# The first expert's row numbers taken from four one-hot tiles of their own, ahead of the routing table

## The chip, the cores and the metric

The kernel runs on one core of one Trainium2 chip. The metric is the device time of one execution in microseconds (us); less is better. The profile is one execution, taken by the hardware profiler, and its times count from the start of its span.

## The reference

Two requests of 256 tokens (512 tokens in four tiles of 128, D = 1024) pass two layers. Layer 0 mixes tokens by a bidirectional mLSTM, layer 1 by a gated short convolution; each mixer is followed by a layer norm, a mixture of experts and another layer norm.

```python
logits = (t @ router_w) + router_b                  # 16 experts in 4 groups of 4
probs = softmax(logits)
g_sel = argmax(sum of the two largest probs of each group)
top_v, top_i = top_k(probs inside group g_sel, 2)
gates = top_v / sum(top_v)
for e in range(16):
    gu = t @ w_gu[e]                                # 1024 -> 512
    h = silu(gu[:, :256]) * gu[:, 256:]
    out += combine[:, e] * (h @ w_down[e])          # 256 -> 1024
x = layer_norm(ALPHA * x + out)
```

## The kernel before

Every large product is made of three products of split operands (hi times hi, hi times lo, lo times hi). ScalarE writes the hi part of a weight unit (128x2048), VectorE the lo part, TensorE multiplies. The experts are computed sparsely: each token has two experts, every expert's tokens are gathered from DRAM into 128 places, multiplied, scaled by their gate and scattered back, and the scattered results are added later.

Between a mixer and its experts stands the router, once a layer. Its steps in order of the engines:

- TensorE ends `out_projection` with `logits(t)` (L710, fp32 products, two instructions each in the trace) and then `spin(6, 5)` (called at L742, recorded as L555). A spin is one product of the identity with 512 columns whose result nobody reads, again two instructions; it only fills TensorE's time.
- VectorE adds constants and takes the maximum (L1649 to L1653), ScalarE the exponential, and VectorE's `choose` finds each token's best group and its two experts with some 28 small instructions (L1671 to L1729). `step_done.wait(but=n)` lets an instruction start before the n latest ones have completed; `step_done.wait()` waits for all. The last one writes `chosen` and releases TensorE (`s_chosen`).
- TensorE's `router` computes every token's place within its experts (L762, L764), then `spin(1, 5)`. VectorE meanwhile writes `values` (token number and result row of every token and expert, L1658) and then reads the places (L1735, L1739).
- VectorE writes eight one-hot tiles of place numbers, one for each choice k and token tile t (L1743); TensorE multiplies each with `values` into a table of the row numbers of all 16 experts (`slot_table`, L779), then runs `spin(2, 5)`.
- VectorE takes the table to `rows_of` (L1748, `s_ix`). GpSimd waits for that and issues indirect DMAs that gather the tokens of expert 0 and expert 1 (L2026), and then weight loads of the next norm. SyncE's queue holds back two expert weight loads and all that follow until gather 0 has landed (L400).
- VectorE computes the gates (L1752 to L1757) and writes them by expert (L1658 again, `s_gv`); TensorE multiplies them with the same one-hot tiles (L779), runs `spin(4, 5)`, and then `tokens_T(0, 0)` transposes the gathered tokens of expert 0 (L795) and the experts begin (L823, later L495 and L852).

TensorE's instructions run in the order in which they are written, so `tokens_T(0, 0)` stands behind the gates' products and the four spins.

Of the kernel before, what the change touches and what calls it, by code (L numbers as in the profile page):

```python
# [5 lines left out]
ALU = mybir.AluOpType  # L6
# [35 lines left out]
def trunk(nc, gate_cols, router_cols, x_prompt, x_sample, router_w, router_b, mlstm_w_in, mlstm_b_gate, mlstm_norm_g, mlstm_w_out,  # L42
# [36 lines left out]
    with ctx:  # L79
        def sb(name, shape, dt=F32):  # L80
            return ctx.enter_context(nc.sbuf_tensor(name, shape, dt))

        def sem(name):
            return ctx.enter_context(nc.semaphore(name))
# [46 lines left out]
        chosen_pad = sb("chosen_pad", [P, 2 * NT + 1, E], F32R)  # L131
        chosen = chosen_pad[:, NT:2 * NT, :]
        place = sb("place", [P, 2, NT])
        facts = sb("facts", [P, 2, NT, 2], F32R)
        shares = sb("shares", [P, 2, NT, 2], F32R)
        r_max = sb("r_max", [P, 1])
# [46 lines left out]
                         for at in (2048, 2304))  # L183
        dn_hi, dn_lo = (of_flat(a)[:, 2048:4096] for a in (xt_hi, xt_lo))
        gate_w_hi, gate_w_lo = (of_flat(a)[:, 0:KC * 16].rearrange("p (k n) -> p k n", k=KC) for a in (h_hi, h_lo))
        zT = temp[:, 0:2048].rearrange("p (b c s) -> p b c s", b=2, c=KC)
        silu_g = temp[:, 1024:1536].rearrange("p (b f) -> p b f", b=2)
        h_tok = temp[:, 1536:2048].rearrange("p (b f) -> p b f", b=2)
# [96 lines left out]
        s_rank = sem("places_multiplied")  # L285
        s_routed = sem("routing_ready")
        s_oh = sem("one_hot_ready")
        s_ixm = sem("rows_multiplied")
        s_gv = sem("gates_by_expert_ready")
        s_gm = sem("slot_gates_multiplied")  # L290
# [200 lines left out]
        def _(pe):  # L491
# [60 lines left out]
            def spin(n, bank):  # L552

                for _ in range(n):
                    pe.matmul(ps[:, bank, :], ident[:, :], ident[:, :].unsqueeze(1).to_broadcast([P, 4, P]),  # L555
                              start=True, stop=True)
# [126 lines left out]
            def out_projection(layer, first_unit, ready, after=lambda kh, t: None):  # L683

                def part(half, kh, t):
                    tok = slice(t * P, (t + 1) * P)
                    for k in range(4):
                        w = slice(k * CG, (k + 1) * CG)
                        x = 4 * kh + k
                        ins = products(ps[:, 4 * half + t, :],  # L690
                                       [(xt_hi[:, x, tok], w_hi[:, kh, w]), (xt_hi[:, x, tok], w_lo[:, kh, w]),
                                        (xt_lo[:, x, tok], w_hi[:, kh, w])],
                                       kh == 0 and k == 0, kh == 1 and k == 3)
                    if t == 3:
                        ins.then_inc(s_hl, 1)
                    elif kh == 1:
                        ins.then_inc(s_bank, 1)

                def raw_T(t, half):
                    pe.wait_ge(s_sum, 2 * NT * layer + (t + 1 if half == 0 else NT + t + 1))  # L700
                    for c in range(4):
                        f0 = (4 * half + c) * P
                        ins = pe.transpose(ps[:, 4 * half + t, c * P:(c + 1) * P], z[:, t, f0:f0 + P], ident[:, :])  # L703
                    ins.then_inc(s_tr, 1)

                def logits(t):
                    for c in range(KC):
                        if c % 4 == 0:
                            pe.wait_ge(s_za, 2 * NT * layer + 2 * t + c // 4 + 1)
                        ins = pe.matmul(ps[:, t, 0:E], zT[:, t % 2, c, :], rout_c[:, layer, c, :],  # L710
                                        start=c == 0, stop=c == KC - 1)
                    ins.then_inc(s_lg, 1)

                for kh in range(2):
                    pe.wait_ge(s_lo, first_unit + kh + 1)
                    for t in range(NT):
                        ready(kh, t)
                        part(0, kh, t)
                        after(kh, t)
                pe.wait_ge(s_lo, first_unit + 3)  # L720
                part(1, 0, 0)
                part(1, 0, 1)
                pe.wait_ge(s_lo, first_unit + 4)
                part(1, 1, 0)
                part(1, 1, 1)
                part(1, 0, 2)
                raw_T(0, 0)
                raw_T(0, 1)
                part(1, 1, 2)
                raw_T(1, 0)  # L730
                raw_T(1, 1)
                logits(0)
                part(1, 0, 3)
                raw_T(2, 0)
                raw_T(2, 1)
                logits(1)
                raw_T(3, 0)
                part(1, 1, 3)
                logits(2)
                raw_T(3, 1)  # L740
                logits(3)
                spin(6, 5)  # L742

            def heads_ready(kh, t):
                pe.wait_ge(s_xtl, 8 + NT * kh + t + 1)
# [12 lines left out]
            def router(layer):  # L758

                pe.wait_ge(s_chosen, layer + 1)  # L760
                out = ps[:, 4, 0:(NT + 1) * E]
                pe.matmul(out, earlier[:, :], slots(NT), start=True, stop=False)  # L762
                for back in range(1, NT + 1):
                    ins = pe.matmul(out, all_ones[:, :], slots(NT - back), start=False, stop=back == NT)  # L764
                ins.then_inc(s_rank, 1)
                spin(1, 5)
                for n in range(2 * NT):
                    pe.wait_ge(s_oh, 2 * NT * layer + n + 1)
                    ins = slot_table(values, 0, n)
                ins.then_inc(s_ixm, 1)  # L770
                spin(2, 5)
                pe.wait_ge(s_gv, layer + 1)
                for n in range(2 * NT):
                    ins = slot_table(gates, 1, n)
                ins.then_inc(s_gm, 1)
                spin(4, 5)
# [562 lines left out]
        def _(dve):  # L1339
            step_done = Steps(dve, s_dve)  # L1340

            def do(ins):

                step_done(ins)
                step_done.wait()
# [318 lines left out]
            def choose(layer):  # L1664
# [48 lines left out]
                                            ALU.is_equal))  # L1713
                step_done.wait(but=1)
                step_done(dve.tensor_reduce(r_most, groups(r_key), AX.X, ALU.max))
                step_done.wait(but=1)
                step_done(dve.tensor_tensor(r_gated[:, 0, :], r_first, r_group, ALU.mult))
                step_done(dve.tensor_tensor(r_gated[:, 1, :], r_second, r_group, ALU.mult))
                step_done.wait(but=2)
                step_done(dve.tensor_tensor(groups(r_tops[:, 1, :]), groups(r_key), wide(r_most, GE), ALU.is_equal))  # L1720
                step_done.wait(but=1)
                step_done(dve.tensor_reduce(top_value[:, :, :].rearrange("p k t -> p (k t)"),
                                            r_gated.rearrange("p k (t g) -> p (k t) g", t=NT), AX.X, ALU.add))
                step_done.wait(but=1)
                for k in range(2):
                    step_done(dve.tensor_tensor(groups(top[:, k].rearrange("p t e -> p (t e)")),
                                                groups(r_tops[:, k, :]), wide(r_group, GE), ALU.mult))
                step_done.wait()
                dve.tensor_tensor(chosen, top[:, 0], top[:, 1], ALU.add).then_inc(s_chosen, 1)  # L1729

                step_done(by_expert(values, facts))

                dve.wait_ge(s_rank, layer + 1)
                rank = ps[:, 4, 0:NT * E].unsqueeze(1).to_broadcast([P, 2, NT * E])
# [1 line left out]
                                                   in1=top[:, :, :, :].rearrange("p k t e -> p k (t e)"),  # L1736
                                                   op0=ALU.add, op1=ALU.mult))
                step_done.wait()
                do(dve.tensor_reduce(place[:, :, :].rearrange("p k t -> p (k t)"),  # L1739
                                     r_rank.rearrange("p k (t e) -> p (k t) e", t=NT), AX.X, ALU.add))  # L1740
                for k in range(2):
                    for t in range(NT):
                        dve.tensor_scalar(one_hot[:, NT * k + t, :], place_no[:, :], place[:, k, t:t + 1], None,  # L1743
                                          ALU.is_equal).then_inc(s_oh, 1)
                do(dve.tensor_reduce(r_max[:, :], ps[:, 4, NT * E:(NT + 1) * E], AX.X, ALU.max))
                dve.tensor_copy(most[:, :], r_max[:, :]).then_inc(s_routed, 1)
                dve.wait_ge(s_ixm, layer + 1)
                dve.tensor_scalar(rows_of[:, :, :], ps[:, 7, 0:2 * E].rearrange("p (e c) -> p e c", c=2), NO_ROW,  # L1748
                                  None, ALU.add).then_inc(s_ix, 1)
                step_done(dve.tensor_copy(last_token[:, :], ps[:, 7, 2 * (E - 1):2 * (E - 1) + 1]))  # L1750

                do(dve.tensor_tensor(r_one[:, :], top_value[:, 0, :], top_value[:, 1, :], ALU.add))  # L1752
                do(dve.reciprocal(r_one[:, :], r_one[:, :]))
                do(dve.tensor_tensor(gate_of[:, :, :], top_value[:, :, :],
# [169 lines left out]
        def _(pool):  # L1924
# [90 lines left out]
            def experts(layer):  # L2015
# [2 lines left out]
                pool.wait_ge(s_tr, 8 * (3 + 2 * layer))  # L2018
                c0 = E * layer

                pool.wait_ge(s_ix, layer + 1)

                def gather(e, j):
                    if e >= 2:
# [8 lines left out]
                                            in_=ye[:, j % 2, :], in_offset=None,  # L2033
                                            bounds_check=last_result, oob_is_err=False).then_inc(s_sca[j % 2], 16)

                for e in range(2):
                    gather(e, e)
                pool.engine_nop().then_inc(s_gi, 1)
                norm_weights(1 + 2 * layer, ln2_g[layer], ln2_b[layer])
                for e in range(2, 4):  # L2040
# [74 lines left out]
```

## Time and profile before

| | us |
|---|---|
| three runs | 872.87, 875.31, 878.15 (median 875.31) |
| the profiled execution | 876.63, of which 874.8 from its first to its last instruction |
| busy of the span | TensorE 851.7, its weight loads 683.8, VectorE 568.2, ScalarE 427.8, GpSimd 128.6 |
| mean granted TensorE clock | 0.991 of 2.4 GHz |

TensorE's busy time includes the spins. A busy engine is not always an engine on the path that sets the end, so the prediction reads the chain of waits and the order of time around the two routers, at about 287 to 302 us (layer 0) and 673 to 689 us (layer 1).

### The profile page before, as it was taken

How to read it: one execution, taken by the hardware profiler on the slowest of the kernel's cores; microseconds unless marked ns; L12 is line 12 of the kernel's file. 1: busy time of each engine (PE TensorE's matmuls, PEld its weight loads, DVE VectorE, ACT ScalarE, POOL GpSimd, SP SyncE). 2: the span in 40 equal slices, each digit the busy share in tenths (PEclk: the TensorE clock that was granted, in tenths of full speed). 3: DMA queues.
4: the chain of work that ended last, by engine and by line, in shares of the span. 5: the costliest groups of instructions: out<-in, count | busy, mean ns of one | idle time of the engine just before them, and what ended most of it. 6: DMA issues, size and time to landing. Idle time of an engine off the chain costs nothing.

```text
span 874.8 us, 9990 instructions
## 1 busy us (share of the span) xinstructions
PE 851.7 (97%) x4004; PEld 683.8 (78%) x4004; DVE 568.2 (65%) x716; ACT 427.8 (49%) x429; POOL 128.6 (15%) x126
## 2 busy tenths in 40 slices
PE   8999999999999999999988999999999999999986
PEld 5888888888888578888864988888887678888853
DVE  4532434356756789999966535425666699999937
ACT  4423222353522388888863131122214288888850
POOL 3300000011400222333210000000000223233110
PEclk9999999999999999999998999999999999999999
DMA  9983313112359399999879322320266699999852
GB/s 347 363 332 97 97 49 97 49 49 96 114 212 372 111 394 344 366 360 331 318 263 393 116 97 97 96 97 1 97 221 260 235 373 345 381 334 353 290 215 105
DMA packets 80834, 193.84 MB, mean 222 GB/s; under 512 B 8249, under 2 KB 8437, under 8 KB 80656
## 3 DMA queue, kind: packets, MB, share of 16 engines
q1 hardware_dynamic: 67344, 159.46, 50.5%
q0 software_dynamic: 13440, 33.69, 10.5%
q8 instruction: 34, 0.56, 0.3%
q14 instruction: 16, 0.13, 0.0%
HBM read 178.95 MB, written 30.43 MB: 239 GB/s over the span
## 4 chain that ended last, share of the span: by engine, by line
PE 90%; DVE 6%; DMA 2%; ACT 2%; issue 1%; POOL 0%; SPq 0%; POOLq 0%; ACTq 0%
PE ps L495 62%; PE ps L852 9%; PE ps L572 4%; PE ps L795 3%; PE ps L622 2%; PE ps L555 2%; PE ps L607 2%; PE ps L823 1%; DVE w_lo L1350 1%; DMA expert_out<-arena,rows_of 1%; PE ps L581 1%; DVE xt_lo L1358 1%; PE ps L710 1%; DVE xt_lo L1785 1%; PE ps L838 1%; PE ps L703 1%
## 5 line engine op out<-in xcount | busy, mean ns | idle before, releaser
L1350 DVE TENSOR_TENSOR w_lo<-arena,w_hi 128x2048 fp32r<-128x2048 f32 x100 | 229.4, 2296 | 126.1 <-ACT w_hi L1036 125.2
L1036 ACT ACTIVATE w_hi<-arena 128x2048 fp32r<-128x2048 f32 x100 | 191.5, 1915 | 158.6 <-PE ps L495 150.6
L495 PE MATMUL ps<-w_hi,xt_hi 128*128 128x512 f32 x480 | 192.4, 401 | 0.0
L495 PE MATMUL ps<-w_hi,xt_lo 128*128 128x512 f32 x480 | 187.4, 390 | 0.0
L495 PE MATMUL ps<-w_lo,xt_hi 128*128 128x512 f32 x480 | 187.1, 390 | 0.0
L495 PE MATMUL ps<-xt_hi,w_hi 128*128 128x512 f32 (+1 forms) x352 | 131.9, 375 | 1.9 <-DVE xt_lo L1358 1.9
L495 PE MATMUL ps<-xt_hi,w_lo 128*128 128x512 f32 (+1 forms) x352 | 130.2, 370 | 0.0
L495 PE MATMUL ps<-xt_lo,w_hi 128*128 128x512 f32 (+1 forms) x352 | 130.1, 370 | 0.0
L495 PEld LDWEIGHTS ps<-w_hi,xt_lo 128*128 128x128 f32 x480 | 90.1, 188 | 19.2
L495 PEld LDWEIGHTS ps<-w_lo,xt_hi 128*128 128x128 f32 x480 | 90.3, 188 | 17.7
L495 PEld LDWEIGHTS ps<-w_hi,xt_hi 128*128 128x128 f32 x480 | 90.2, 188 | 17.5
L2032 POOL DMA_INDIRECT expert_out<-arena,rows_of x30 | 58.4, 1945 | 181.2 <-ACT arena L1221 181.2
L495 PEld LDWEIGHTS ps<-xt_hi,w_hi 128*128 128x128 f32 x352 | 66.3, 188 | 13.3 <-DVE xt_lo L1358 2.1
L2026 POOL DMA_INDIRECT arena<-x_of_experts,rows_of x32 | 35.1, 1097 | 281.9 <-DVE rows_of L1748 248.2
L495 PEld LDWEIGHTS ps<-xt_hi,w_lo 128*128 128x128 f32 x352 | 66.3, 188 | 11.5
L495 PEld LDWEIGHTS ps<-xt_lo,w_hi 128*128 128x128 f32 x352 | 66.3, 188 | 11.2
L1785 DVE TENSOR_TENSOR xt_lo<-arena,xt_hi 128x2048 fp32r<-128x2048 f32 x30 | 68.8, 2293 | 5.7 <-ACT xt_hi L1207 5.7
L1207 ACT ACTIVATE xt_hi<-arena 128x2048 fp32r<-128x2048 f32 x30 | 57.5, 1918 | 16.6 <-PE ps L852 16.6
L1188 ACT ACTIVATE xt_hi<-ps 128x1024 fp32r<-128x1024 f32 x32 | 32.9, 1028 | 23.1 <-PE ps L795 23.1
L1769 DVE TENSOR_TENSOR xt_lo<-ps,xt_hi 128x1024 fp32r<-128x1024 f32 x32 | 38.9, 1214 | 1.1 <-ACT xt_hi L1188 1.1
L2000 POOL TENSOR_TENSOR arena<-arena,ln_g 128x512 f32<-128x512 f32 x8 | 11.4, 1424 | 166.7 <-ACT arena L1097 166.5
L1501 DVE TENSOR_TENSOR temp<-ps,temp 128x256 f32<-128x256 f32 (+1 forms) x32 | 9.2, 349 | 40.7 <-PE ps L607 22.3
(239 smaller groups left out, 1021.1 us busy)
## 6 DMA issues: line engine op xcount, KB each, us to landing
arena<-in_moe_w_gu SPq DMA_DIRECT2D x64, 1024.0 KB, 15.4
arena<-in_moe_w_down SPq DMA_DIRECT2D x32, 1024.0 KB, 16.8
arena<-in_mlstm_w_in SPq DMA_DIRECT2D x16, 1024.0 KB, 7.2
arena<-in_conv_w_in SPq DMA_DIRECT2D x12, 1024.0 KB, 11.9
expert_out<-ln_b POOLq DMA_DIRECT2D x8, 1024.0 KB, 13.8
arena<-expert_out SPq DMA_DIRECT2D x16, 512.0 KB, 7.9
arena<-in_mlstm_w_out SPq DMA_DIRECT2D x4, 1024.0 KB, 5.1
x_of_experts<-arena SPq DMA_DIRECT2D x8, 512.0 KB, 10.4
```

What stands on the lines that cost most here:

```text
L495: ins = pe.matmul(out, a, b, start=first and n == 0, stop=last and n == 2)
L572: pe.matmul(ps[:, 2 * t + half, :], ident[:, :], y_back[t][:, k, half * CG:(half + 1) * CG], start=False, stop=False)
L795: ins = pe.transpose(ps[:, c // 4, (c % 4) * P:(c % 4 + 1) * P], xg[:, j % 2, c * P:(c + 1) * P], ident[:, :])
L852: ins = pe.matmul(ps[:, 5 + half, :], a[:, k, :], w[:, at], start=first and k == 0, stop=last and k == 1)
L1036: act.activation(w_hi[:, parity, :], raw(slot), ACT.Copy).then_inc(s_hi, 1)
L1188: act.activation(xe_hi[:, j % 2, :, :], ps[:, 0:2, :].rearrange("p b (c s) -> p (b c) s", c=4), ACT.Copy).then_inc(s_ghi, 1)
L1207: act.activation(dn_hi, raw(3 * j + 2), ACT.Copy).then_inc(s_dhi, 1)
L1350: dve.tensor_tensor(w_lo[:, parity, :], raw(slot), w_hi[:, parity, :].bitcast(F32), ALU.subtract).then_inc(s_lo, 1)
L1769: dve.tensor_tensor(xe_lo[:, j % 2, :, :], ps[:, 0:2, :].rearrange("p b (c s) -> p (b c) s", c=4), xe_hi[:, j % 2, :, :].bitcast(F32), ALU ...
L1785: dve.tensor_tensor(lo, raw(3 * j + 2), hi.bitcast(F32), ALU.subtract).then_inc(s_dlo, 1)
L2026: pool.indirect_dma_start(out=xg[:, j % 2, :], out_offset=None, in_=source, in_offset=bass.IndirectOffsetOnAxis(rows_of[:, e, 0:1], 0), bo ...
L2032: pool.indirect_dma_start(out=target, out_offset=bass.IndirectOffsetOnAxis(rows_of[:, e, 1:2], 0), in_=ye[:, j % 2, :], in_offset=None, bo ...
```

## The change

Expert 0 gets its row numbers by a way of its own. `first_place` is each token's place in expert 0 (or 0), `first_values` its row numbers for expert 0; four one-hot tiles `first_hot`, one for each token tile, are multiplied with them in fp32 into a bank of their own, and VectorE takes the result to `rows_of[:, 0]` after the third of the eight old one-hot tiles. `s_ix` is raised twice a layer: the first releases gather 0, the second gather 1. In `choose`, the two gated values move behind `chosen` and their reduction behind the table, the two merges of choice and group become one, and three partial waits become full. The spins ahead of the router go from six to five.

```diff
+        first_hot = temp[:, 0:512].rearrange("p (t s) -> p t s", t=NT)
...
-                spin(6, 5)
+                spin(5, 5)
...
                 spin(1, 5)
+                for t in range(NT):
+                    pe.wait_ge(s_foh, NT * layer + t + 1)
+                    ins = pe.matmul(ps[:, 6, 0:2], first_hot[:, t, :], first_values[:, t, :], start=t == 0,
+                                    stop=t == NT - 1)
+                ins.then_inc(s_fix, 1)
...
                 step_done(dve.tensor_reduce(r_most, groups(r_key), AX.X, ALU.max))
-                step_done.wait(but=1)
+                step_done.wait()
+                step_done(dve.tensor_tensor(groups(r_tops[:, 1, :]), groups(r_key), wide(r_most, GE), ALU.is_equal))
+                step_done.wait()
+                step_done(dve.tensor_tensor(
+                    top[:, :, :, :].rearrange("p k t (g e) -> p k (t g) e", e=GE),
+                    r_tops.rearrange("p k (g e) -> p k g e", e=GE),
+                    r_group.unsqueeze(1).unsqueeze(3).to_broadcast([P, 2, NT * NG, GE]), ALU.mult))
+                step_done.wait()
+                dve.tensor_tensor(chosen, top[:, 0], top[:, 1], ALU.add).then_inc(s_chosen, 1)
+
+                step_done(by_expert(values, facts))
                 step_done(dve.tensor_tensor(r_gated[:, 0, :], r_first, r_group, ALU.mult))
                 step_done(dve.tensor_tensor(r_gated[:, 1, :], r_second, r_group, ALU.mult))
                 step_done.wait(but=2)
-                step_done(dve.tensor_tensor(groups(r_tops[:, 1, :]), groups(r_key), wide(r_most, GE), ALU.is_equal))
-                step_done.wait(but=1)
-                step_done(dve.tensor_reduce(top_value[:, :, :].rearrange("p k t -> p (k t)"),
-                                            r_gated.rearrange("p k (t g) -> p (k t) g", t=NT), AX.X, ALU.add))
-                step_done.wait(but=1)
-                for k in range(2):
-                    step_done(dve.tensor_tensor(groups(top[:, k].rearrange("p t e -> p (t e)")),
-                                                groups(r_tops[:, k, :]), wide(r_group, GE), ALU.mult))
-                step_done.wait()
-                dve.tensor_tensor(chosen, top[:, 0], top[:, 1], ALU.add).then_inc(s_chosen, 1)
-
-                step_done(by_expert(values, facts))
+                step_done(dve.tensor_tensor(first_values[:, :, :], values[:, 0:NT, 0, :].bitcast(F32),
+                                            values[:, NT:2 * NT, 0, :].bitcast(F32), ALU.add))
...
-                do(dve.tensor_reduce(place[:, :, :].rearrange("p k t -> p (k t)"),
-                                     r_rank.rearrange("p k (t e) -> p (k t) e", t=NT), AX.X, ALU.add))
+                per_expert = r_rank.rearrange("p k (t e) -> p k t e", t=NT)
+                step_done(dve.tensor_tensor(first_place[:, :], per_expert[:, 0, :, 0], per_expert[:, 1, :, 0],
+                                            ALU.add))
+                step_done(dve.tensor_reduce(place[:, :, :].rearrange("p k t -> p (k t)"),
+                                            r_rank.rearrange("p k (t e) -> p (k t) e", t=NT), AX.X, ALU.add))
+                step_done.wait(but=1)
+                for t in range(NT):
+                    dve.tensor_scalar(first_hot[:, t, :], place_no[:, :], first_place[:, t:t + 1], None,
+                                      ALU.is_equal).then_inc(s_foh, 1)
+                step_done.wait()
                 for k in range(2):
                     for t in range(NT):
                         dve.tensor_scalar(one_hot[:, NT * k + t, :], place_no[:, :], place[:, k, t:t + 1], None,
                                           ALU.is_equal).then_inc(s_oh, 1)
+                        if k == 0 and t == 2:
+                            dve.wait_ge(s_fix, layer + 1)
+                            dve.tensor_scalar(rows_of[:, 0, :], ps[:, 6, 0:2], NO_ROW, None, ALU.add
+                                              ).then_inc(s_ix, 1)
...
-                dve.tensor_scalar(rows_of[:, :, :], ps[:, 7, 0:2 * E].rearrange("p (e c) -> p e c", c=2), NO_ROW,
+                dve.tensor_scalar(rows_of[:, 1:E, :], ps[:, 7, 2:2 * E].rearrange("p (e c) -> p e c", c=2), NO_ROW,
                                   None, ALU.add).then_inc(s_ix, 1)
                 step_done(dve.tensor_copy(last_token[:, :], ps[:, 7, 2 * (E - 1):2 * (E - 1) + 1]))
+                do(dve.tensor_reduce(top_value[:, :, :].rearrange("p k t -> p (k t)"),
+                                     r_gated.rearrange("p k (t g) -> p (k t) g", t=NT), AX.X, ALU.add))
...
-                pool.wait_ge(s_ix, layer + 1)
+                pool.wait_ge(s_ix, 2 * layer + 1)
...
-                for e in range(2):
-                    gather(e, e)
+                gather(0, 0)
+                pool.wait_ge(s_ix, 2 * layer + 2)
+                gather(1, 1)
```

## Rows read from the trace of the kernel before

**Rows 1.** The page, part 4: the chain that ended last, by engine

```profile
PE 90%; DVE 6%; DMA 2%; ACT 2%; issue 1%; POOL 0%; SPq 0%; POOLq 0%; ACTq 0%
```

**Rows 2.** Chain in order of time, router of layer 0 (start, us, what)

```profile
293.75 1.66 PE ps L779 x8
295.40 1.81 PE ps L555 x4
...
298.17 3.53 PE ps L555 x8
301.70 0.89 PE ps L795 x8
```

**Rows 3.** Chain in order of time, router of layer 1

```profile
679.77 1.65 PE ps L779 x8
681.42 3.51 PE ps L555 x4
...
685.73 3.53 PE ps L555 x8
```

**Rows 4.** Waits of TensorE, 300 to 450 us, the longest of four

```profile
PE ps L838 <- DVE temp L1776: 1.2, 1, 1.2
```

**Rows 5.** Queue of SyncE in order of time: first expert loads behind gather 0

```profile
300.81 14.45 SPq L356 DMA_DIRECT2D arena<-in_moe_w_gu  x6
...
686.88 15.97 SPq L356 DMA_DIRECT2D arena<-in_moe_w_gu  x6
```

**Rows 6.** VectorE in order of time, router of layer 0 (start, busy, line)

```profile
290.75 0.22 DVE L1715 TENSOR_REDUCE temp<-temp 128x16 f32<-128x64 f32 x1
...
291.05 0.22 DVE L1720 TENSOR_TENSOR temp<-temp 128x64 f32<-128x64 f32 x1
291.19 0.18 DVE L1722 TENSOR_REDUCE top_value<-temp 128x8 f32<-128x32 f32 x1
291.30 0.36 DVE L1726 TENSOR_TENSOR top<-temp 128x64 f32<-128x64 f32 x2
291.69 0.22 DVE L1729 TENSOR_TENSOR chosen_pad<-top 128x64 fp32r<-128x64 f32 x1
...
292.76 0.29 DVE L1735 SCALAR_TENSOR_TENSOR temp<-ps,top 128x128 f32<-128x128 f32 x1 [0.51 <-PE ps L764]
293.09 0.29 DVE L1739 TENSOR_REDUCE place<-temp 128x8 f32<-128x128 f32 x1
293.41 1.66 DVE L1743 TENSOR_SCALAR xt_hi<-place_no,place 128x128 fp32r<-128x128 f32 x8
...
295.44 0.19 DVE L1748 TENSOR_SCALAR rows_of<-ps 128x32 uint32<-128x32 f32 x1
...
296.62 0.43 DVE L1658 TENSOR_TENSOR xt_lo<-top,shares 128x256 fp32r<-128x256 f32 x1
```

**Rows 7.** TensorE in order of time, layer 0, before the router

```profile
284.73 1.92 PE L710 MATMUL ps<-rout_c,temp 128*128 128x16 f32 x16
286.50 5.40 PE L555 MATMUL ps<-ident 128*128 128x512 f32 x12
291.97 0.31 PE L762 MATMUL ps<-chosen_pad,earlier 128*128 128x80 f32 x1
```

**Rows 8.** VectorE, 530 to 620 us, groups by shape

```profile
L1909 DVE TENSOR_TENSOR arena<-ps,arena 128x512 f32<-128x512 f32 x8 | 5.2, 684 | 2.6 <-PE ps L495 2.6
...
L1898 DVE TENSOR_SCALAR arena<-arena,taps 128x512 f32<-128x512 f32 x8 | 3.9, 486 | 0.3
```

**Rows 9.** GpSimd in order of time, first gather of layer 0

```profile
296.49 1.09 POOL L2026 DMA_INDIRECT arena<-x_of_experts,rows_of  x1 [59.55 <-DVE rows_of L1748]
```

**Rows 10.** VectorE in order of time, layer 1: gates by expert

```profile
682.70 0.42 DVE L1658 TENSOR_TENSOR xt_lo<-top,shares 128x256 fp32r<-128x256 f32 x1
```

**Rows 11.** Busy time by stretch; behind POOL the granted clock, DMA share, GB/s

```profile
291.90:295.30 3.40, 3.24 (x16) 2.34 (x16) 2.79 (x14) 0.00 (x0) 0.00 (x0) 1.00 0.03 5
...
681.30:684.70 3.40, 3.40 (x6) 1.40 (x6) 1.55 (x9) 0.00 (x0) 1.93 (x2) 0.51 0.14 17
```

More of the change, by code:

```diff
@@ L133, in trunk @@
         place = sb("place", [P, 2, NT])
+        first_place = sb("first_place", [P, NT])
+        first_values = sb("first_values", [P, NT, 2])
         facts = sb("facts", [P, 2, NT, 2], F32R)
@@ L287, in trunk @@
         s_oh = sem("one_hot_ready")
+        s_foh = sem("first_one_hot_ready")
+        s_fix = sem("first_rows_multiplied")
         s_ixm = sem("rows_multiplied")
```

## The prediction

> **What bounds the kernel.** I read the chain by engine first: 90% of it is TensorE [rows 1]. So a change in the routers counts only as far as it moves what TensorE does next. The second view is the chain in order of time around the router of layer 0: table products, two spins (to 297.21), the gates' products, four spins from 298.17, and the transposes of expert 0 at 301.70, with no gap between them [rows 2]. The reader is to see that the piece ahead of the transposes is spins, not the gather. The third view says how late the gather is: SyncE's first load behind gather 0 goes out at 300.81 in layer 0 and 686.88 in layer 1 [rows 5], so gather 0 has landed by then. The transposes start at 301.70, and at 689.26 in layer 1 (685.73 + 3.53) [rows 2, 3]. The gather has 0.89 us to spare in layer 0 and 2.38 in layer 1. Last, TensorE's waits among the experts: the longest is 1.2 us, on VectorE, none on a DMA [rows 4], and layer 1 has the same one. What comes late at the first transposes stays late to the end.
>
> **The change part by part**, in layer 0, against the profiled execution (876.63 us).
>
> *Up to `chosen`.* Before, L1715 starts at 290.75 and L1729 at 291.69 [rows 6]. Now L1720 waits for all of L1715 (0.22) and starts at 291.00, since a full wait adds some 0.03 (L1739 starts 293.09, is busy 0.29, L1743 starts 293.41) [rows 6]. It ends at 291.22. The one merge of 128x128 starts at 291.25; by L1735 and L1739 (0.29 at that size) it ends at 291.54, and `chosen` starts at 291.57: 0.12 earlier. Bounds: 0.36 for the merge, as for the two it replaces, gives 0.05 earlier; nothing excludes that its broadcast is slower still, which would cost 0.1 or so.
>
> *The sixth spin.* Twelve instructions take 5.40 us and end at 291.90; the places' product begins at 291.97 [rows 7]. With `chosen` 0.12 earlier the sixth spin would be in the way by about 0.05. Without it TensorE ends at 291.0 and idles for 0.85 us. Worth nothing by itself, but the idle time matters below.
>
> *Behind `chosen`.* Two gated values and `first_values` are three small instructions. Starts there are 0.11 to 0.14 apart (L1720, L1722, L1726), so 0.3 to 0.4 us; the idle time of 0.51 ahead of L1735 hides them [rows 6]. Cover gone, they would cost at most the difference, none here. L1735 starts at 292.64.
>
> *First places and one-hot tiles.* `first_place` (some 0.08 apart from the next), then L1739 at 293.04. The first tiles wait for `first_place` alone, so they start at 293.25 instead of 293.41. Eight tiles take 1.66, that is 0.2 each [rows 6]; four cost 0.8, and the old tiles begin at 294.07: 0.66 late. Three of them run to 294.7. TensorE needs four fp32 products meanwhile: 16 instructions of L710 take 1.92, 0.12 each [rows 7], so eight take under 1.0 but follow the tiles, the last at about 293.9 + 0.28. From the end of the last old tile (293.41 + 1.66 = 295.07) to L1748 at 295.44 lie 0.37 [rows 6]; with a second pass 0.49. So `s_fix` comes at about 294.65, just before VectorE gets to it. `rows_of[:, 0]` starts at 294.7 and costs 0.1 in the row. What is queued behind this wait are five old tiles, and so the table, the rows of 15 experts and the gates: if the products are slower, all of that is late by as much. Sum at the table: 0.66 + 0.05 + 0.1 = 0.8 late; L1748 starts at 296.25.
>
> A row with an f32 result speaks for cheaper tiles: L1898 takes 486 ns where L1909 takes 684 for 512 elements [rows 8], 0.4 ns an element, so 0.05 less per 128-element tile and 0.2 for four. But then `s_fix`, tied to TensorE's passes, comes last, and I keep 0.8; 0.6 is the lower end. The Trainium skill (VectorE: DVE Perf Modes, Mode 2×_2P) says that an fp32 scalar operation between SBUF tiles makes two results a cycle; by it the tiles would cost about half their streaming time less, and the sum would be the same lower end.
>
> *Gather 0.* L1748 starts at 295.44 and ends at 295.63; the gather starts at 296.49 [rows 6, 9]. Now `rows_of[:, 0]` ends at 294.85 and the gather starts at about 295.7, 0.78 earlier, and lands at 300.0. Gather 1 waits for the second `s_ix` (296.45), which is there before gather 0 has been issued (296.8). All of this lies behind the spins: worth nothing. SyncE's loads go out 0.78 earlier, also for nothing, since no engine waits for them [rows 4]. There is a rule that speaks against the change: the Trainium skill (SBUF — State Buffer, SBUF: two separate sides) says that a DMA issued from GpSimd can't write its descriptors while VectorE runs such a two-port operation. Gather 0 now starts beside the last old tile (until 295.9), so it could be 0.2 later; that is inside its spare time, and the sum stays.
>
> *Gates.* The reduction of `top_value` moves between table and gates: 0.18 + 0.03 = 0.21 [rows 6]. The gates by expert, at 296.62 before, start 0.81 + 0.21 = 1.02 late and release TensorE at 298.1. TensorE's two spins behind the table end at 297.21 + 0.81 = 298.02, so the gates decide. The four spins and the transposes follow unchanged: **1.02 us late in layer 0**.
>
> In layer 1 the two spins took 3.51 instead of 1.81, at a granted clock of 0.51 [rows 2, 3, 11], the 1.2 GHz level. There they end at 684.93, long after the gates at 683.12 [rows 3, 10], so only the table's shift counts: **0.81 us**.
>
> *The clock.* From the table's products to the four spins it took 5.96 us in layer 1 and 4.42 in layer 0 [rows 2, 3]: the fall cost 1.54. Ahead of it TensorE had waited for `chosen`, run one spin, and followed VectorE's tiles; layer 0 did the same and kept 1.00 [rows 11]. So the stretch stands at the edge. Between the long spins it lasted 3.5 us (291.90 to 295.40); now it lasts 5.0 (291.0 to 296.05), with the same one spin inside. I take it that the clock falls in both layers: **1.54 more**, bounds -1.54 (in neither) and some 3.5 above (below).
>
> Sum: 1.02 + 0.81 + 1.54 = 3.4 us, 880.0 against 876.63. The profiled execution was 1.32 above the median of the runs, so against 875.31 the forecast is **878.7**.
>
> **Rivals.**
> 1. *One fall or none.* If the clock falls as often as before, 1.83: 877.1. If in neither layer, 2 × 1.02 - 1.54 = 0.5: 875.8. For it: layer 0 showed none. Against it: the stretch is 1.5 us longer.
> 2. *Slower by over 0.5%.* The clock falls earlier or stays low longer, so that the first products (pace 0.12 each, doubled) hold VectorE up, or the four spins run at the low level too. Spins at that level took 1.7 more for 1.81; four would take 3.5 more: 882.2. It decides from 1.0 us of such time on (0.5% of 875.31 is 4.4, 879.7). For it: TensorE does less for longer. Against it: the one fall seen ended when the two spins had run.
> 3. *The earlier gather pays.* If the transposes had waited for the gather after all, 0.78 a layer would be gained: 873.7. For it: 0.89 to spare in layer 0 is little. Against it: the spins run without a gap to the transposes, and 2.38 to spare in layer 1. Even so the four spins stand behind later gates.
> 4. *The first rows come no sooner.* If `s_fix` comes half a microsecond later than worked out, the gather starts only 0.3 earlier and all behind the wait is 0.5 later, twice: 879.7. For it: the two ends stand 0.05 apart. Against it: the eight passes fit between the tiles.
>
> **How the numbers follow.** Forecast 0.45, one fall 0.2, none 0.1, rival 2 0.18, rival 3 0.04, rival 4 0.03. The runs of before spread from 872.87 to 878.15, and half a per cent is about what a measurement can tell from no change. Of the forecast some three tenths may be measured above 879.7; with rival 2 and a share of rival 4 slower has 0.32, rival 3 and spread leave 0.03 for faster. The range takes in the case without a fall and ends between forecast and rival 2: 875.2 to 881.8.
>
> **What would show it.** Right: gather 0 starts some 0.8 us sooner relative to `chosen` and the first loads too; the gates by expert start 1.0 later; the chain still shows spins ahead of the transposes; a granted clock near 0.5 behind both tables. Wrong: transposes at the same distance from `chosen` or nearer; a wait of VectorE at `rows_of[:, 0]` of over 0.2 us; TensorE waiting on a DMA among the experts.

## The result, and the profile after

| | us | mean granted clock, executions |
|---|---|---|
| before, ten runs | median 877.12 (872.87 to 878.43) | not listed |
| after, ten runs | median 882.84 (878.23 to 886.02) | 0.9844 |
| after, ran again beside 29 runs of before | median 882.53 (before 875.88) | 0.9847 (before 0.9916) |

The change makes the kernel slower: the ratio is 1.0081 (95% interval 1.006 to 1.0102), and 1.0078 (1.0055 to 1.0101) beside more runs of before. (A ratio is that of its own measurement and not exactly the quotient of two medians.) The forecast was 878.7 with a range up to 881.8: the direction was right, the size too small.

The profiled execution of after took 878.23 us, the shortest of its ten. Its trace shows what happens, and too little of how often: its mean granted clock is 0.989, that of the other nine 0.981 to 0.989. So the lines below are read for the mechanism, and the size comes from the executions.

The first view is the page's chain that ended last, by engine, of after. It answers to [rows 1]: still TensorE.

```profile
PE 91%; DVE 5%; ACT 1%; DMA 1%; issue 1%; POOL 0%; SPq 0%; POOLq 0%; ACTq 0%
```

The second is the chain in order of time of after, router of layer 0 and, behind the dots, of layer 1 (start, us, what). It answers to [rows 2, 3]. L774 are the new products of the first rows, L789 the table's and the gates' products, L560 the spins, L805 the transposes of expert 0 (L767 and L769, the places, lie between the first two rows).

```profile
289.38 3.94 PE ps L560 x8
...
294.78 1.05 PE ps L774 x8
...
296.28 1.17 PE ps L789 x5
297.45 3.40 PE ps L560 x4
300.85 0.80 PE ps L789 x8
301.65 3.53 PE ps L560 x8
305.18 0.89 PE ps L805 x8
...
682.41 1.21 PE ps L789 x5
683.62 3.17 PE ps L560 x4
686.79 0.80 PE ps L789 x8
687.59 3.53 PE ps L560 x8
```

The reader is to see the two spins behind the table: 3.40 us in layer 0, where they took 1.81 before [rows 2], and 3.17 in layer 1, where they took 3.51 [rows 3]. The granted clock says why. These are rows of the busy time by stretch of after (behind POOL the granted clock, DMA share, GB/s): the two stretches of those spins, and then 26 us around each router.

```profile
297.40:300.80 3.40, 3.40 (x7) 1.49 (x7) 1.67 (x9) 0.00 (x0) 2.76 (x4) 0.54 0.34 85
683.40:686.80 3.40, 3.40 (x9) 1.61 (x8) 1.63 (x10) 0.00 (x0) 2.84 (x4) 0.58 0.33 85
284.00:310.00 26.00, 25.67 (x105) 16.26 (x105) 19.17 (x68) 6.83 (x9) 4.30 (x5) 0.87 0.44 143
674.00:700.00 26.00, 24.84 (x97) 15.51 (x97) 17.81 (x64) 8.28 (x10) 5.34 (x6) 0.93 0.62 209
```

At 0.54 and 0.58 most of both stretches runs at the 1.2 GHz level: the clock falls behind both tables. Over 26 us, 0.93 stands for 3.6 us at half clock (0.07 × 26 × 2), and 0.87 for 6.8. Layer 0 has a second fall ahead of its router: the last spins there are slow (289.38 to 293.32), and hold the places' product back by 0.9 us after `chosen`. No changed instruction has run by then, and e8 and e9, kernels without first tiles, show such a fall too, so it isn't the change's own. It makes layer 0 a bad measure of the change: the one-hot tiles start 2.26 us behind `chosen` there and 1.67 in layer 1.

VectorE in order of time, router of layer 1 of after, answers to [rows 6, 10]:

```profile
678.91 0.22 DVE L1734 TENSOR_TENSOR chosen_pad<-top 128x64 fp32r<-128x64 f32 x1
...
680.58 0.86 DVE L1756 TENSOR_SCALAR temp<-place_no,first_place 128x128 f32<-128x128 f32 x4
681.36 0.67 DVE L1761 TENSOR_SCALAR xt_hi<-place_no,place 128x128 fp32r<-128x128 f32 x3
682.00 0.16 DVE L1765 TENSOR_SCALAR rows_of<-ps 128x2 uint32<-128x2 f32 x1
682.08 1.06 DVE L1761 TENSOR_SCALAR xt_hi<-place_no,place 128x128 fp32r<-128x128 f32 x5
...
683.66 0.19 DVE L1770 TENSOR_SCALAR rows_of<-ps 128x30 uint32<-128x30 f32 x1 [0.25 <-PE ps L789]
...
685.06 0.43 DVE L1668 TENSOR_TENSOR xt_lo<-top,shares 128x256 fp32r<-128x256 f32 x1
```

The first rows (L1765) carry no wait. The gates by expert (L1668) start 6.15 us behind `chosen`, in [rows 6] 4.93: 1.22 later. GpSimd's first gather of layer 1 of after answers to [rows 9]; SyncE's first loads behind it, and TensorE's longest wait between 303 and 450 us, answer to [rows 5, 4].

```profile
682.98 1.08 POOL L2050 DMA_INDIRECT arena<-x_of_experts,rows_of  x1 [187.81 <-DVE rows_of L1765]
```

```profile
687.36 13.50 SPq L361 DMA_DIRECT2D arena<-in_moe_w_gu  x5
```

```profile
PE ps L848 <- DVE temp L1800: 1.2, 1, 1.2
```

The gather starts 4.07 us behind `chosen` instead of 4.80, and the loads 8.45 instead of about 9.1. All of that stands behind the four spins, and the longest wait of TensorE among the experts is the 1.2 of before. The gain that the change brings is there and is worth nothing. The gates by expert are ready at 685.49 (685.06 + 0.43), and TensorE comes to their products only at 686.79, behind the slow spins: where the clock falls, the spins cover the later gates.

### The profile page after: what moved, and what is told of

Its sections match the earlier page's. It is cut to its first block, busy times and chain, and to the rows that moved or that the text cites. A ratio compares the mean times of both kernels' runs of the same rounds, so it can differ in the third digit from the quotient of the medians.

```text
span 876.1 us, 10026 instructions
## 1 busy us (share of the span) xinstructions
PE 853.8 (97%) x4016; PEld 687.6 (78%) x4016; DVE 570.5 (65%) x728; ACT 428.0 (49%) x429; POOL 128.1 (15%) x126
## 4 chain that ended last, share of the span: by engine, by line
PE 91%; DVE 5%; ACT 1%; DMA 1%; issue 1%; POOL 0%; SPq 0%; POOLq 0%; ACTq 0%
PE ps L500 62%; PE ps L862 9%; PE ps L577 3%; PE ps L805 3%; PE ps L560 3%; PE ps L627 2%; PE ps L612 2%; PE ps L833 1%; PE ps L715 1%; DVE w_lo L1360 1%; PE ps L586 1%; DVE xt_lo L1809 1%; PE ps L708 1%; PE ps L848 1%; DVE xt_lo L1368 1%
```

## The experiments

Two theories went in. **P**: the stretch with first tiles and their small products lets the clock fall. **S**: the missing sixth spin does. Each run is compared with runs of before on the same chip. The kernels of the first group are e1 to e4, of the second e5 to e8, of the third e9 to e11. Mean clocks are over the executions that the ratios use; before had 0.9924, 0.9916 and 0.9928 in the three groups. "At equal clock" means that a difference of mean clock between a kernel and before in its group has been taken off, at 0.79 us for 0.001. That figure is one slope for all executions of all these kernels, with a level of its own for each kernel; they scatter by some 0.95 us around it, so a distance at equal clock is good to some 0.3 us.

**e1_six_spins**: after, with the sixth spin back.

```diff
-                spin(5, 5)
+                spin(6, 5)
```

> The changed kernel with the sixth spin ahead of the router back. Theory P (the longer chain of tiles and gates costs 1.8 us, and the rest of the loss is the clock falling more often because TensorE has little to do for longer around the tiles): the loss stays nearly whole, ratio to before 1.006 to 1.009. Theory S (the clock falls because TensorE now idles 0.85 us ahead of the router): ratio 1.001 to 1.003, the 1.8 us of the chain alone being left.

Median 879.71 against 875.17, ratio 1.005 (1.0025 to 1.0074), mean clock 0.9902. It lies between the theories: the sixth spin gives back part. Its trace has one router without a fall, and one with a long one. The chain of layer 0 of this kernel:

```profile
298.39 3.60 PE ps L560 x4
302.00 1.52 PE ps L789 x8
303.51 5.60 PE ps L560 x8
```

Here not only the two spins are slow, but also the gates' products (1.52 for 0.80) and the four spins (5.60 for 3.53).

**e2_spin_between**: after, with one spin between the first products and the table's.

```diff
                 ins.then_inc(s_fix, 1)
+                spin(1, 5)
```

> The changed kernel with one more spin between the products of the first rows and those of the table, where TensorE follows the one-hot tiles anyway; it should delay the chain by 0.3 us a layer at most. P: the clock falls less often behind the table, ratio to before 1.002 to 1.005, so 2 to 5 us under the changed kernel. S: no change against the changed kernel, 1.007 to 1.010.

Median 877.36, ratio 1.0034 (1.0006 to 1.0061), clock 0.9916, as P expected. Neither router of its trace falls behind the table. The gates by expert still start 6.26 us behind `chosen`, 1.33 later than before, and with no slow spins to cover them they are what TensorE waits for (chain of layer 1):

```profile
683.03 0.43 DVE xt_lo L1669
...
683.50 1.07 PE ps L790 x8
```

**e3_regroup_alone**: before, with the regrouped operations of `choose`, the moved reduction and five spins, without first tiles.

```diff
-                spin(6, 5)
+                spin(5, 5)
...
+                step_done(dve.tensor_tensor(
+                    top[:, :, :, :].rearrange("p k t (g e) -> p k (t g) e", e=GE),
...
-                for k in range(2):
-                    step_done(dve.tensor_tensor(groups(top[:, k].rearrange("p t e -> p (t e)")),
```

> The kernel before with the router operations regrouped and five spins, without tiles and products of the first expert. P: chain 0.1 us a layer either way, stretch between the long spins 0.9 us longer by the idle time: ratio 0.999 to 1.003. S: the clock loses as in the change: 1.004 to 1.007.

Median 876.92 of eleven executions (a twelfth took 2207.81 us and is left out), ratio 1.0021 (0.9988 to 1.0055), clock 0.9895. The ratio is what P expected; the interval reaches into what S expected, so this run alone doesn't decide.

**e4_first_alone**: before, with first tiles, their products and the two releases of `s_ix`, but the old `choose` and six spins.

```diff
+                for t in range(NT):
+                    pe.wait_ge(s_foh, NT * layer + t + 1)
+                    ins = pe.matmul(ps[:, 6, 0:2], first_hot[:, t, :], first_values[:, t, :], start=t == 0,
+                                    stop=t == NT - 1)
...
+                        if k == 0 and t == 2:
+                            dve.wait_ge(s_fix, layer + 1)
```

> The kernel before with tiles and products of the first expert alone; router operations as before, six spins. The chain is late by about 0.9 us a layer. P: ratio to before 1.005 to 1.009, nearly the whole loss. S: 1.002 to 1.003.

Median 878.81, ratio 1.0047 (1.0021 to 1.0072), clock 0.9897. That is just under P's figure and above S's; the interval takes in all of S's and part of P's. So far: neither part brings all of it, and both lower the clock. The second group took up that they add.

**e5_change_again**: after, unchanged, beside the others of its group.

```diff
(no edit)
```

> The changed kernel itself, beside the others of this group and with a second trace. Over the runs so far an execution takes 0.78 us more for every 0.001 that its mean granted clock is lower; at one and the same clock the change stands 1.2 us above before. Theory C (a chain 1 to 2 us longer, and the rest is time at the low clock level): median 5 to 7 us above before, mean clock 0.984 to 0.986 against 0.992 of before, and the trace shows a stretch at the low level around each router, at least one of them reaching into the four spins behind the gates. Theory D (the loss is in the chain, the clock the same): mean clock like before's.

Median 882.53 against 875.88, ratio 1.0078 (1.0055 to 1.0101), clock 0.9847, as expected. This trace is more like most executions than the first one of after (882.26 us, clock 0.985). Its chain of layer 1, and then the same stretch by granted clock:

```profile
684.38 3.60 PE ps L560 x4
687.99 1.52 PE ps L789 x8
689.50 5.68 PE ps L560 x8
```

```profile
683.20:686.60 3.40, 3.40 (x8) 2.17 (x9) 2.55 (x15) 0.00 (x0) 2.54 (x3) 0.54 0.17 43
686.60:690.00 3.40, 3.40 (x11) 2.38 (x10) 0.46 (x2) 0.00 (x0) 0.73 (x2) 0.50 0.69 243
690.00:693.40 3.40, 3.40 (x5) 1.35 (x4) 3.40 (x2) 0.00 (x0) 0.00 (x0) 0.50 0.86 312
...
284.00:310.00 26.00, 25.67 (x106) 16.12 (x106) 19.23 (x68) 6.83 (x9) 4.30 (x5) 0.87 0.43 144
674.00:700.00 26.00, 24.84 (x82) 14.43 (x82) 16.71 (x63) 5.98 (x7) 4.31 (x5) 0.80 0.55 201
```

TensorE is busy 3.40 of 3.40 us in each of three stretches, and the clock stays at half through all of them. Over both routers 0.87 and 0.80 make 6.8 and 10.4 us at half clock, where the trace of before has one fall of some 3.5 in layer 1 and none in layer 0 [rows 11].

**e6_six_and_between**: after, with both spins.

```diff
-                spin(5, 5)
+                spin(6, 5)
...
                 ins.then_inc(s_fix, 1)
+                spin(1, 5)
```

> The changed kernel with the sixth spin back and one more spin between the first products and the table. C: mean clock 0.993 to 0.996, ratio to before 1.000 to 1.003, the longer chain alone being left. D: ratio like the change's, 1.006 or more.

Median 877.02, ratio 1.0002 (0.998 to 1.0023), clock 0.9934, as expected. The chain of its layer 1, and the granted clock of the stretch:

```profile
680.88 1.05 PE ps L774 x8
681.93 0.96 PE ps L560 x2
682.89 0.81 PE ps L790 x8
...
686.67 3.53 PE ps L560 x8
```

```profile
682.90:685.60 2.70, 2.60 (x12) 1.30 (x11) 2.06 (x13) 0.00 (x0) 2.32 (x3) 1.00 0.16 33
```

Two spins more, and the whole loss of time is gone: in layer 1 the clock holds 1.00 up to the gates, and in layer 0 it fell ahead of the router but not behind the table. The first tiles and late gates remain. The clock is even above before's (0.9916): at equal clock e6 stands 2.0 us above before, so a gain in clock stands here against a longer chain that is still there.

**e7_one_spin_behind_gates**: e6, with one spin instead of four behind the gates (theory **G**: those spins only hold up what the earlier gather has ready).

```diff
-                spin(4, 5)
+                spin(1, 5)
```

> As the one before it, with one spin in place of four between the gates' products and the transposes of expert 0. Theory G (the earlier gather was worth nothing because four spins stood behind the gates): the transposes now wait for gather 0 or come right behind the one spin, 1.5 to 2.5 us earlier a layer; 3 to 5 us under the kernel with four spins, ratio to before 0.995 to 0.999. Rival H (the spins are not what the transposes wait for, or leaving them out costs as much by the clock): within 1 us of the kernel with four.

Median 872.77, ratio 0.9971 (0.9948 to 0.9993), clock 0.9947. As G expected, that is 4.25 us under e6, from which it differs by this edit alone. Of the 3.1 us between its mean and that of before, 2.4 go with the higher clock. In layer 1 the next wait shows at once, on VectorE (TensorE in order of time, first products of the experts):

```profile
692.43 1.19 PE L834 MATMUL ps<-w_hi,xt_lo 128*128 128x512 f32 x4 [0.76 <-DVE xt_lo L1794]
```

**e8_before_three_spins**: before, with three spins behind the gates, to see whether that alone pays.

```diff
-                spin(4, 5)
+                spin(3, 5)
```

> The kernel before with three spins in place of four behind the gates. G: the transposes come 0.86 us earlier a layer, up to the landing of the gather; 1.7 us less, ratio 0.997 to 0.999. H: no change, 0.9995 to 1.001.

Median 875.78, ratio 0.9992 (0.9969 to 1.0014), clock 0.991. Inconclusive: one spin of 0.88 a layer is too little for this measurement.

**e9_no_inner_spin**: before, without the one spin between places and table, which takes work out and adds none.

```diff
-                spin(1, 5)
```

> The kernel before without the one spin that stands between the places' product and the table: no instruction of any chain is longer, TensorE only does less in the stretch between the long spins. C (the clock falls because TensorE does less there, and a fall costs 1.5 to 4 us): falls in both layers nearly always, mean clock 0.985 to 0.989, 3 to 6 us above before. D (the chain alone sets the loss): as before, within 1 us.

Median 878.88 against 874.98, ratio 1.004 (1.0017 to 1.0062), clock 0.9872, 3.9 us above before as C expected: the clock alone costs, without first tiles and without a late gate. That both layers fall nearly always isn't shown: behind the table of its trace only layer 1 fell (layer 0 fell ahead of its router). The chain of layer 1 shows the same long fall (1.84 for the table's products, then spins of 3.60 and 5.50):

```profile
681.95 1.84 PE ps L778 x8
683.79 3.60 PE ps L555 x4
687.39 1.52 PE ps L778 x8
688.91 5.50 PE ps L555 x8
```

**e10_before_one_spin**: before, with one spin instead of four behind the gates.

```diff
-                spin(4, 5)
+                spin(1, 5)
```

> The kernel before with one spin in place of four behind the gates. G: the gather lands 0.9 us ahead of the transposes in layer 0, so it is the next bound: 1 to 2 us under before, ratio 0.997 to 0.999, the earlier gather of the change being what would let this go further. If the first rows are worth nothing even then, as much as with the change and one spin: 0.997. H: no change.

Median 874.64, ratio 1.0008 (0.9989 to 1.0027), clock 0.9905: the gain that was expected isn't there in the time. The clock is lower than before's 0.9928, and at equal clock e10 stands 1.4 us below before, as G expected. Whether the clock is lower because the spins are missing, no run shows. With the spins gone, the transposes wait for the gather in both layers (TensorE in order of time):

```profile
301.08 1.09 PE L795 MATMUL ps<-ident,arena 128*128 128x128 f32 x8 [1.64 <-DMA arena<-x_of_experts,rows_of]
...
682.82 1.09 PE L795 MATMUL ps<-ident,arena 128*128 128x128 f32 x8 [1.37 <-DMA arena<-x_of_experts,rows_of]
```

From the start of `chosen` to the transposes it took 9.08 and 8.85 us in this trace, in that of before 9.85 in layer 0 and, with a fall, 11.38 in layer 1.

**e11_one_spin_swapped**: e7, with two of VectorE's first units exchanged with the lo part that TensorE waited for.

```diff
                 units(0, 0, 0)
-                units(0, 0, 1)
                 gathered_lo(0, 0)
+                units(0, 0, 1)
```

> The changed kernel with the sixth spin, the spin between and one spin behind the gates, in which VectorE also takes the lo part of expert 0's tokens before that of the second weight unit. In the trace with one spin TensorE waits for that lo part until 307.26 us, behind two weight units of 2.24 us each. If that wait is the next bound: 2 us a layer less, 3 to 4 us under the kernel with one spin, ratio to before 0.992 to 0.994. Rival: the second half then waits for the second weight unit and gives it back, within 1 us of 0.997.

Median 873.3, ratio 0.9986 (0.9968 to 1.0005), clock 0.9918: not the gain that was expected. The edit does what it says. The chain of its layer 1 goes from one spin straight to the transposes and to the products, with no wait on VectorE:

```profile
681.87 0.95 PE ps L560 x2
682.83 0.89 PE ps L806 x8
...
684.81 3.01 PE ps L834 x12
```

The transposes come 8.59 us behind `chosen` in both layers, nearest of all. That e11 measured no less than e7 goes with the clock, 0.9918 against 0.9947, a difference that stands for 2.3 us. At equal clock e11 is 2.4 us below before and e7 0.7, which is about half of what the swap was expected to bring; this is worked out, not run.

## Why the prediction was wrong

**What bounds the kernel**: right. TensorE heads the chain, and the earlier gather is hidden by the spins. Only e10, with three of them gone, makes TensorE wait for a gather.

**Up to `chosen`**: forecast 0.12 earlier; 0.10 measured.

**The sixth spin**, "worth nothing by itself": right as to the path, and the text left its idle time for the clock. It seems worth part of the loss, 1.005 with it (e1) against 1.0081 without, but these intervals overlap.

**First tiles**: `rows_of[:, 0]` didn't wait, as worked out. Four f32 tiles took 0.78 us (680.58 to 681.36), 0.195 each; the fp32r tiles behind `rows_of[:, 0]` took 0.196 each. So f32 tiles were no cheaper, and the lower end of 0.6 was no lower end. Whether an fp32 scalar operation between SBUF tiles makes two results a cycle, as the Trainium skill (VectorE: DVE Perf Modes, Mode 2×_2P) states, these rows of one size and of the same operation don't tell.

**Gather 0**: forecast 0.78 earlier and worth nothing; 0.73 earlier relative to `chosen`, worth nothing. Its issue took 1.08 (682.98 to 684.06), and 1.09 before [rows 9]. Only the first 0.16 us of it ran beside the last one-hot tile (until 683.14). So the delay by descriptors of which the Trainium skill warns (SBUF — State Buffer, SBUF: two separate sides) was hardly put to the test.

**Gates**: forecast 1.02 later against the start of the router, 1.14 relative to `chosen`; 1.22 measured, and 1.33 in e2. Right, and so is the price of a chain without slow spins: 2 × 1.02 by the prediction, 2.1 us in e2 and 2.0 in e6 at equal clock, two kernels whose traces show no slow spin behind the table. Where the clock falls, the slow spins cover part of it. The prediction saw that for layer 1 and yet counted 1.02 for layer 0, where it let the clock fall too; by its own rule both layers cost 0.81, so its sum was 0.21 too high. In the group of e5, the mean of after (882.56) lies 6.4 us above that of before (876.13), of which the clock (0.9847 against 0.9916) makes 6.9 × 0.79 = 5.5, and 0.9 remains. Some 0.3 of this lies outside the instructions: an execution of after takes 2.15 us more than from its first to its last instruction, one of before 1.81.

**The clock** is the step that failed, in its size. It said that "the clock falls in both layers: **1.54 more**", that is one fall more, over when the two spins have run, by the only fall that it read in before's routers. At the routers, the profiled execution fits that: its transposes start 12.82 and 12.05 us behind the start of `chosen`, with 9.85 and 11.38 before; less 0.1 twice, for the `chosen` that comes earlier, that is 2.9 and 0.6 us, with 2.56 and 0.81 forecast. Part of that is luck: 0.6 of the 2.9 come from the fall ahead of layer 0's router (2.26 instead of 1.67 to the one-hot tiles), which the forecast didn't have. And it was the shortest of ten. In e5's trace the same kernel has 12.82 and 15.35: the second fall lasted through the gates' products and the four spins. That is the second mechanism of rival 2; its price for it, 3.5 us, was 2.9 here (5.68 for 3.53 and 1.52 for 0.80), so that its total of 882.2 lies this near the median is in part luck. I argued against it with one observation: that "the one fall seen ended when the two spins had run". Falls that last through the four spins are in four traces (e1, e3, e5, e9), two of them of kernels without first tiles. And one such fall stood in the trace of before, outside the routers: behind the experts of layer 0 the clock went to half at about 459.5 us and came back at 466.3, with TensorE busy without a gap from 461 on (busy time by stretch of before; the stretches at the dots show 0.50 too):

```profile
460.00:461.00 1.00, 0.48 (x1) 0.50 (x2) 0.00 (x0) 1.00 (x1) 0.00 (x0) 0.50 0.90 344
...
465.00:466.00 1.00, 1.00 (x3) 0.48 (x2) 0.00 (x0) 0.00 (x0) 0.00 (x0) 0.50 1.02 416
466.00:467.00 1.00, 1.00 (x3) 0.40 (x3) 0.00 (x0) 0.00 (x0) 0.00 (x0) 0.85 1.03 414
```

That is 6.8 us at half clock in one fall, about twice the 3.5 on which the price rested. In time at half clock the forecast had one fall of 3.5 us more; 0.0069 of 875 us, at a half, are 12.1 us. In the sum, the clock made 5.5 instead of 1.54. Where the 12.1 us lie is known from the traces alone: around the two routers e5 has 13.6 us more than before, 3.4 of them ahead of layer 0's router, where no changed instruction has run.

**From the profiled execution to the median**: the 1.32 taken off stands. The ten runs of before have a median of 877.12, but the three groups of 29 to 35 runs have 875.17, 875.88 and 874.98, near the 875.31 that was used. What the forecast lacks, 3.4 against 6.4 to 7.1 (1.0081), is the clock's, and the chain gave a little of it back.

**What lowers the clock.** Behind the table, routers of kernels with first tiles and no spin between them and the table (after, e1, e4, e5) fell in 6 of 8 cases; with that spin (e2, e6, e7, e11) in 0 of 8; without first tiles (before, e3, e8, e10) in 3 of 8, and in 1 of 2 where the old spin is missing too (e9). These are small counts, of one trace a kernel. e6 against e5 shows that two spins take the loss away, and e9 that a spin less, with nothing added, brings about half of it. Neither P nor S seems right alone: each of e1 and e2 gives part back (0.9902 and 0.9916 of mean clock against 0.9844 of after), and both spins together all. How the loss divides between the two stays open; the intervals of e1, e2 and e4 overlap.

**Left open, too**: whether earlier first rows are worth anything once the four spins are gone. e7 (0.9971, 0.9948 to 0.9993) and e10 (1.0008, 0.9989 to 1.0027) differ by them, but also by the regrouped operations, one spin and the group that they ran in, and at equal clock they turn round (0.7 and 1.4 us below before). In the traces TensorE waits for the gather only without them (1.64 and 1.37 us in e10). The transposes come 8.59 to 10.05 us behind `chosen` with them, 8.85 to 9.08 without; the 10.05 are e7's, with a fall ahead of both routers.

## What to carry to other kernels

Before work is brought forward, look at what stands in order behind the wait that it would shorten: here four spins, which had to go before an earlier gather could count. Where TensorE gets small products spread over a longer stretch, price a fall of the clock by the mean granted clock of many executions, not by the one fall that one profile happens to hold; one filler product in the right gap (between the first products and the table) costs 0.1 us there (gates at 6.26 instead of 6.15), and no trace with it has a fall behind the table. A profile is one draw: see where its time and its clock stand among the other executions before its sum is carried over to their median.

## What was not expected of the hardware

Once at the 1.2 GHz level, the clock stayed there for some 10 us (683.2 to 693.4 in e5) while TensorE was busy without a gap, and in the trace of after it came back within about 3.4 us, in the same code. Executions of one kernel differ mostly by such time: after has clocks from 0.981 to 0.989 and times from 878.23 to 886.02. And 0.001 of mean clock costs 0.79 us of a possible 0.87 (0.001 × 875, at which every us at half clock would lose half a us of path), so nearly all of the slow time stands on the path.
